# A hybrid decoder trunk whose mixer takes its steps from a written-out table instead of a planner

## The reference

```python
def mixer(h, conv_gdn_buf, sconv_buf, s0, segments, w_in, w_out, conv_gdn, conv_sc, a_log, dt_bias, gdn_norm):
    proj = h @ w_in
    qkv = silu(causal_dw_conv(concat([conv_gdn_buf, proj[..., OFF_Q:OFF_Z]]), conv_gdn))
    q, k = l2_normalize(q) * GDN_DK ** -0.5, l2_normalize(k)
    beta, g = sigmoid(b_raw), -exp(a_log) * softplus(a_raw + dt_bias)
    for length, chunk in segments:
        o_seg, s = gdn_chunks(q[:, sl], k[:, sl], v[:, sl], beta[:, sl], g[:, sl], s, chunk)
    o = o * rsqrt(mean(o * o) + NORM_EPS) * gdn_norm * silu(z)
    u = gate_c * h_in
    y_sc = gate_b * causal_dw_conv(concat([sconv_buf, u]), conv_sc)
    return concat([o, y_sc]) @ w_out, s, new_conv_gdn, new_sconv
```

## Time and profile before

| | |
|---|---|
| median of 3 runs | 1502.56 us (1497.63 to 1502.75) |
| the profiled execution | 1502.63 us, span 1500.8 us |
| PE busy | 1456.8 us, 97% |
| DVE busy | 866.9 us, 58% |
| ACT busy | 620.3 us, 41% |
| PE busy from 266 to 500 us (mixer, layer 0) | 226.78 of 234 us |
| PE busy from 1024 to 1248 us (mixer, layer 1) | 216.79 of 224 us |
| mean granted TensorE clock | 0.983 |

### The profile page before, as it was taken

How to read it: one execution, slowest core, us unless ns; L and a number is a source line. 1 busy time by engine, 2 the same in 40 slices (tenths; PEclk the granted TensorE clock), 3 DMA queues, 4 the chain that set the end, 5 groups by cost and what they waited for, 6 DMA issues and landing times.

```text
span 1500.8 us, 22849 instructions
## 1 busy us (share of the span) xinstructions
PE 1456.8 (97%) x9628; PEld 1417.3 (94%) x9628; DVE 866.9 (58%) x1448; ACT 620.3 (41%) x980; POOL 36.3 (2%) x124
## 2 busy tenths in 40 slices
PE   9999998999999999999999999999999999999997
PEld 8999998889989999999999999998799899999997
DVE  5655434876367665553376554347763776655433
ACT  5443333553324453333354433346532244544432
POOL 0000001010000000000000000010100000000000
PEclk9999999999999999999999999999999999999999
DMA  6544344221114334434435443442211143444342
GB/s 244 200 141 141 125 141 156 85 85 61 58 57 157 109 138 149 142 130 135 159 127 197 141 141 125 151 145 85 85 62 57 57 177 108 146 146 163 125 151 97
DMA packets 49461, 191.24 MB, mean 127 GB/s; under 512 B 6000, under 2 KB 8432, under 8 KB 48848
## 3 DMA queue, kind: packets, MB, share of 16 engines
q1 hardware_dynamic: 48752, 184.66, 35.9%
q0 software_dynamic: 608, 5.12, 0.8%
HBM read 183.33 MB, written 6.43 MB: 126 GB/s over the span
## 4 chain that ended last, share of the span: by engine, by line
PE 90%; DVE 5%; ACT 3%; issue 1%; DMA 1%; SPq 0%; ACTq 0%; DVEq 0%
PE PS L1402 25%; PE PS L1404 24%; PE PS L1403 24%; PE PS L1561 5%; PE PS L1442 2%; PE PS L1443 2%; PE PS L1447 2%; DVE WL L997 2%; PE PS L1559 1%; PE PS L1727 1%; DVE CV L1127 1%; ACT WH L728 1%; PE PS L1679 1%; PE PS L1596 0%; DMA RAW<-in_w_in 0%
## 5 line engine op out<-in xcount | busy, mean ns | idle before, releaser
L1402 PE MATMUL PS<-XH,WH 128*128 128x336 f32 (+1 forms) x1728 | 555.1, 321 | 6.3 <-DVE WL L997 6.3
L1404 PE MATMUL PS<-XH,WL 128*128 128x336 f32 (+1 forms) x1728 | 544.7, 315 | 0.0
L1403 PE MATMUL PS<-XL,WH 128*128 128x336 f32 (+1 forms) x1728 | 544.5, 315 | 0.0
L997 DVE TENSOR_TENSOR WL<-RAW,WH 128x1024 fp32r<-128x1024 f32 (+1 forms) x312 | 398.5, 1301 | 195.5 <-ACT WH L728 195.5
L728 ACT ACTIVATE WH<-RAW 128x1024 fp32r<-128x1024 f32 (+1 forms) x312 | 343.1, 1118 | 201.8 <-DMA RAW<-in_w_down 171.5
L1402 PEld LDWEIGHTS PS<-XH,WH 128*128 128x128 f32 x1728 | 326.0, 189 | 27.2 <-issue 24.3
L1403 PEld LDWEIGHTS PS<-XL,WH 128*128 128x128 f32 x1728 | 326.3, 189 | 0.0
L1404 PEld LDWEIGHTS PS<-XH,WL 128*128 128x128 f32 x1728 | 326.0, 189 | 0.0
L1402 PE MATMUL PS<-HH,WH 128*128 128x336 f32 (+1 forms) x704 | 221.0, 314 | 0.0
L1404 PE MATMUL PS<-HH,WL 128*128 128x336 f32 (+1 forms) x704 | 220.4, 313 | 0.0
L1403 PE MATMUL PS<-HL,WH 128*128 128x336 f32 (+1 forms) x704 | 220.2, 313 | 0.0
(11 more groups left out here) (232 smaller groups left out, 1331.3 us busy)
## 6 DMA issues: line engine op xcount, KB each, us to landing
RAW<-in_w_up SPq DMA_DIRECT2D x176, 512.0 KB, 4.2
RAW<-in_w_down SPq DMA_DIRECT2D x64, 704.0 KB, 4.1
RAW<-in_w_in SPq DMA_DIRECT2D x56, 512.0 KB, 4.2
RAW<-in_w_out SPq DMA_DIRECT2D x16, 512.0 KB, 4.7
SEQ_S<-in_states SPq DMA_DIRECT2D x2, 2048.0 KB, 10.2
out_state_s<-SEQ_S POOLq DMA_DIRECT2D x2, 2048.0 KB, 7.7
X<-in_x SPq DMA_DIRECT2D x8, 168.0 KB, 4.1
out_y<-X SPq DMA_DIRECT2D x4, 320.0 KB, 2.3
```

The source lines that it names most:

```text
L997: dve.tensor_tensor(WL[slot][:, cols], RAW[slot][:, cols], WH[slot][:, cols].bitcast(F32), ALU.subtract).then_inc(split_lo.sem, 1)
L1402: pe.matmul(out, wh, xh, start=first, stop=False)
L1403: pe.matmul(out, wh, xl, start=False, stop=False)
L1404: return pe.matmul(out, wl, xh, start=False, stop=last)
```

## The change

The planner is removed, and the list is written out: `HEAD` holds what stands ahead of the first part of tile 4, and row n of `BEHIND_PART` (72 rows) what stands behind the n-th part. The set of steps is the same, step for step; no operation, shape, buffer or semaphore changes. `delta_groups`, which counts the small products and gives them their banks, reads the new list, so the products take another turn round the three banks.

```diff
-LAG = 2
-PER_SLOT = 2
...
-def delta_stages():
...
+HEAD = [
+    ("entry",), ("gate_rows",), ("evac", 0), ("evac", 1), ("gate_read",), ("tap", 0), ("tap", 1), ("gate_cols",), ("evac", 2),
+]
...
+BEHIND_PART = [
+    [("evac", 3), ("tap", 2), ("hi", 1, 0), ("conv", 0)],
...
 def mixer_steps():
...
+    steps = list(HEAD)
+    for now, work in enumerate(BEHIND_PART):
+        steps.append(("part", FIRST_TILE + now // PARTS, now % PARTS))
+        steps += work
+    return steps
```

More of the change, by code:

```diff
@@ L81 @@
 PART_KT = [(0, 3), (3, 6), (6, KT)]
-LAG = 2
-PER_SLOT = 2
-NO_PRODUCTS = ("unit", "o_inv", "o_low", "spread", "mirror")
-BEHIND = ("rob", "o_inv", "o_low")
-READ_AT, OUT_AT = 38, 49
 TILES = [("qkv", n) for n in range(6)] + [("z", 0), ("qkv", 6), ("qkv", 7), ("z", 1), ("qkv", 8), ("z", 2), ("qkv", 9), ("z", 3),
```

172 lines of the change are left out of this document (75 added, 97 removed), and 3 rows, old and new, of the table BEHIND_PART.

## The result

The changed kernel takes 1477.93 us (median of 4 runs, 1477.32 to 1479.72), against 1501.62 us for the kernel before (4 runs, 1497.63 to 1502.75). The ratio is 0.9849, 95% interval 0.9828 to 0.987: 1.5% faster. The profiled execution took 1479.72 us, its span is 1477.9 us, the mean clock 0.987.

The account below looks back on a forecast made before the run. PE, busy 97% of the span, was taken as the bound. Per layer, 10.5 us removed (7.1 waits, 3.4 clock) less 3.4 added gave 7.1, 14.2 in all: 1502.63 to 1488.4 us, range 1481.5 to 1498.

Parts of the forecast that it names:

- the ceiling: Mixer: most that any reordering can gain, 7.1 us of PE waits plus 3.4 us of clock, 10.5 us a layer.
- (a): `gate_cols` directly behind `gate_rows`: PE waits while the rows pass DVE, 0.7 us a layer, between 0.5 and 1.0.
- (b): `x 1 2` directly behind `nt 1`: PE waits for ACT's copy, 0.9 us a layer, between 0.7 and 1.2.
- (c): `sq_rows 4` in the row behind tile 7: PE comes 0.4 us too early for ACT's squares, between 0 and 1.5.
- (d): Behind tile 11: DVE is later than PE, two bank waits (`x 2 2`, `kk 1`), 0.5 us, between 0 and 2.
- (f): `o 0` three products behind `sn 0 0`: an added wait of 0.2 us a layer.
- (e): Mixer's end, `conv 25` and `lo 13 0` later: DVE's last split late for `out_o`, 0.7 us, between 0 and 2.
- The removed waits: Mixer: PE's waits at tile 6, the squares, `nt 0`, `sn`, `gb 1` and `kt 2` all go, 7.1 us a layer.
- both falls: Clock drops behind tile 6's wait and near 375 us: both go, 1.7 us each, 3.4 us a layer.
- rival 1: Mixers: the clock's falls stay or come elsewhere, four at 1.7 us, 6.8 us, giving 1495.2 us; chance 0.18.
- rival 2: Behind 11.1, 16.1 and 24.1: DVE's lumped work delays PE, 14.4 us in both layers, giving 1502.8 us; chance 0.14.
- rival 3: Last four tiles: DVE's own waits delay `out 0`; slower kernel, 1510.4 us at 11 us a layer; chance 0.05.

Follow-up runs that it names:

- e9: Changed kernel plus 20 unused products a layer of `sq_rows` shape, four in a row in each of tiles 8 to 12: 1505.05 us.
- e10: Changed kernel plus 20 unused products a layer of `sq_rows` shape, each alone between two weight matmuls: 1513.25 us.
- e13: Changed kernel with `sn 1 0` and `mirror 1 32` swapped, so `sn 1 0` stands apart from `sn 1 1`: 178.41 us from gates to `out_o`, layer 0.
- e8: Changed kernel with five rows' products merged into neighbouring rows and `x 1 2` moved behind the next part: 1476.38 us, ratio 0.9835.
- e3: Kernel before with only `conv 15` moved behind `x 0 8` and `y 1 4` in its row: 1495.88 us in one run.
- e14: Changed kernel with the split `lo 1 0` moved behind `conv 3`, putting back the wait ahead of tile 6: 1486.8 us in one run.
- e1: Changed kernel's rows up to the one behind part 2 of tile 10, the old order from there on: 1487.78 us, ratio 0.9919.
- e12: Kernel before with only `conv 15` moved last in its row, profiled and timed a second time: 1500.32 us over 10 runs, ratio 0.9993.
- e11: Kernel before, unchanged, profiled once more: 1500.11 us in one run.
- e7: Changed kernel with five rows' products merged into neighbouring rows, five places fewer: 1479.64 us, ratio 0.9858.

## Why the prediction was wrong

**The step that failed is the ceiling: "So the ceiling of any reordering is 10.5 us a layer ... Nothing below can bring more."** All 10.48 us of it went, 1.28 us of new waits came, and 11.65 us were gained, so 2.45 us came from what was taken as fixed: PE's time at full clock outside the listed waits. Two things were wrong in that. First, I had priced a step by its kind, as if a matmul's cost did not depend on its neighbours. A product over 336 columns costs 0.29 us more alone between weight matmuls than in a row with its like (e9, e10), and an `sn` at most 0.33 (e13). Second, I took a wait at its listed length, and it costs 0.07 to 0.24 us more, about 0.9 us a layer over the waits that went. Both could be seen in the rows: `sq_rows` was put at 0.65 us without asking what the matmuls around it took, and the 2.46 us between two starts at tile 6 stood beside the listed 2.15. The lower end of the range rested on the ceiling, so the range could not hold the result.

**The added waits** were predicted at 3.4 us a layer and are 1.28.
- (a) `gate_cols` behind `gate_rows`: 0.7 predicted, 0.59 measured.
- (b) `x 1 2` behind `nt 1`: 0.9 predicted, 0.69 measured. The transposes take 0.60 us there, and ACT's copy began at 347.72; e8 takes the wait away.
- (c) `sq_rows 4`, (d) the two bank waits behind tile 11, (f) `o 0`: 0.4, 0.5 and 0.2 predicted; the view lists none.
- (e) The end: 0.7 predicted, 0 measured. DVE's timeline has the split of the last operand at 464.77 for 1.20 us, to 465.97, and PE asks for it at 466.11. The cover is 0.14 us.

```profile
464.77 1.20 DVE L1291 TENSOR_TENSOR XL<-BY,XH 128x1008 fp32r<-128x1008 f32 x1
```

So the sum fails by 2.1 us a layer here and by 2.45 at the ceiling, 9.1 us in both layers. The profiled execution is 1488.4 - 1479.72 = 8.7 us under the forecast. With the waits right and the ceiling kept, the forecast would have been 1484.2.

**The removed waits** all went. Two readings of the list behind that were wrong and did no harm. `sq 7` stands one part ahead of its sum and not two; ACT still ended it at 317.85, 1.1 us before PE asked. And only two of the eight `sn`, not four, stand as a pair. The walk to tile 6 had ACT's `hi 1 0` done 6.8 us behind the gates' last product (288.3 against 281.49); it was done 6.6 us behind it (289.48 against 282.88). Tile 6 was put at 9.9 us behind it and came at 9.96.

**The table load.** The changed kernel's rows have 1.28 us and the next activation 0.01 us later. The extra drain that the Trainium skill (ScalarE: Activation LUTs, What ACT_TABLE_LOAD costs) adds to every switch is not seen, and the 0.8 us that it would have left ahead of tile 6 are not there.

**The clock.** That both falls go was right (0 in both mixers, in layer 1 too). That each can be had back at 1.7 us was right only in this company: in the old order the first cost the stage nothing, since `sq_rows 2` waited for its squares either way (e3), and it counted here because the squares came earlier too. The reason was half right. With the long wait put back a fall came back behind it, in both layers (e14), though in e3 the same wait had none. The second fall was not the wait's own: e1 has the wait without it, e12 had a fall elsewhere. Nor are the falls a fixed sum: the profile that I added up had four in its mixers, e11, the same kernel, three. Against rival 1 I had argued that "old waits of 0.77 us had no fall behind them". One profile could not carry that: e12 has a fall where none had been, with no wait above 0.83 us near it. The Trainium skill (TensorE: Matmul & The Clock Gate, A second HAM failure mode: psum-queue depth-cycling) has frequent short idle times make the clock swing. The traces agree in part: in the new order, with two waits of 0.6 and 0.7, the clock never fell in a mixer; in the old, with nine, it did in both profiles, and in e3, with ten, it did not.

**Other figures.** The waits of layer 1 are as long as those of layer 0 (7.06 and 7.07 us) and not 0.6 us longer; a wait of 0.6 us for RC behind the mixer may have been counted with them. The upper ends of (a) to (f) add up to 7.9 us a layer and not 7, which gives 1497.4 and not 1495.6, still inside the range.

**The rivals.** None came. DVE's lumps (rival 2) delayed nobody by an amount that the view lists, and at the end (rival 3) PE never waited.

## What to carry to other kernels

Listed waits and clock losses are no ceiling for a reordering of a full engine. Compare the time between starts on both sides of a switch or a wait, not the duration of an instruction or the listed idle time, before calling the rest fixed. And losses do not simply add: behind one that goes, the next engine's lateness may appear in its place, as at e3's `sq_rows 2`. Check such a reading with extra products, joined and apart; the sum over both sides of the switch was 0 for one shape and 0.29 us for another. Do not judge an order by the falls of one profile: an unchanged kernel showed three and four of them, and an edit that gained less than could be told over 10 runs looked 4 us faster in its first.

## What was unexpected of the hardware

- One product of 128 columns between weight matmuls hands over after 0.14 us, and the weight matmul behind it takes 0.24 instead of 0.154: together nothing (0.08 us over 20 places). One of 336 columns and 8 output rows costs 0.29 us more alone than in a row (15 places, e9 and e10).
- A listed wait of 0.17 us cost 0.41 us from start to start (e7, at 454.44).
- A fall of the clock in a mixer took 1.70 us of PE's time each time, but the stage lost between nothing (before, the first) and 1.6 us (e14: 182.42 - 177.71 - 3.12). It came behind 9 of 12 waits of 2.1 to 3.1 us, and an identical order had it in one run and not in another.
- Outside the stages the clock is at 0.50 near 260, 500, 750, 1000 and 1240 us in the profile of every kernel. These falls differ in length from profile to profile: near 500 us they cost 3.4 us in the kernel before and 1.7 us in the same kernel's second profile (e11).
